# A hybrid layer's 32 experts: the home of weight tiles changes from 12 fixed tiles to a ring of 16

## What is computed

```python
def moe_ffn(h, w_router, b_router, w_gu, b_gu, w_down, b_down):
    logits = (h @ w_router + b_router).astype(F32)
    top_val, top_idx = lax.top_k(logits, TOP_K)          # TOP_K = 4
    gate = jax.nn.softmax(top_val, axis=-1)
    ...
    def expert_block(args):
        xb, e = args
        gu = xb @ w_gu[e] + b_gu[e]                      # 1024 x 2048
        gt = jnp.minimum(gu[:, :D_FF], SWIGLU_LIMIT)
        up = jnp.clip(gu[:, D_FF:], -SWIGLU_LIMIT, SWIGLU_LIMIT)
        act = gt * jax.nn.sigmoid(SWIGLU_ALPHA * gt) * (up + 1.0)
        return act @ w_down[e] + b_down[e]               # 1024 x 1024
```

## Time and profile before

| what | value |
|---|---|
| median of 3 runs | 1384.24 us (1382.01 to 1384.98) |
| profiled execution, its own time | 1385.36 us |
| its span on the core | 1383.4 us, mean granted TensorE clock 0.985 |
| PE busy | 1306.0 us, 94% |
| DVE, ACT, POOL busy | 465.5, 211.8, 20.8 us |
| moved by DMA | 440.18 MB, 318 GB/s over the span |
| expert refills | from 434.69 us on |

### The profile page before, as it was taken

The page is one execution under the profiler, slowest core; times in us unless marked ns, Lnnn a source line. Parts: engine busy times, 40 slices in busy tenths (PEclk is TensorE's granted clock), DMA queues, the critical chain, the costliest instruction groups (busy, mean ns, idle before and its releaser), DMA issues.

```text
span 1383.4 us, 21763 instructions
## 1 busy us (share of the span) xinstructions
PE 1306.0 (94%) x8567; PEld 582.1 (42%) x8567; DVE 465.5 (34%) x983; ACT 211.8 (15%) x556; POOL 20.8 (2%) x30
## 2 busy tenths in 40 slices
PE   5999989999998999999999999999999999999997
PEld 4677544467644343334333333333333333333332
DVE  2454153352535332233222332222332222233223
ACT  3541232460332000000000000000000000000000
POOL 0000010200000000000000000000000000000000
PEclk9999979999998999999999999999999999999999
DMA  9511000365105899999999999999999999999996
GB/s 335 194 62 63 1 28 16 152 219 208 69 6 208 344 422 422 422 422 422 422 422 422 422 422 422 422 422 422 422 422 422 422 422 422 422 422 422 422 421 276
DMA packets 75064, 440.18 MB, mean 318 GB/s; under 512 B 10147, under 2 KB 12681, under 8 KB 25782
## 3 DMA queue, kind: packets, MB, share of 16 engines
q1 hardware_dynamic: 74940, 439.64, 77.7%
q10 hardware_dynamic: 90, 0.06, 0.0%
HBM read 436.35 MB, written 3.33 MB: 318 GB/s over the span
## 4 chain that ended last, share of the span: by engine, by line
PE 50%; DMA 43%; DVE 3%; ACT 2%; issue 1%; SPq 1%; POOL 0%; DVEq 0%; POOLq 0%; ACTq 0%
PE bank L983 47%; DMA weights<-in_w_gu 42%; PE bank L986 2%; SPq L494 1%; ACT weights L572 1%; ACT scaled L572 1%; DMA x<-in_x_sample 0%; ACT stream L572 0%; DVE x L2252 0%; DVE x L2095 0%; POOL stats L545 0%; ACT hT L572 0%; DVE scaled L1698 0%; DVE x L1694 0%; DVE stream L1694 0%
## 5 line engine op out<-in xcount | busy, mean ns | idle before, releaser
L983 PE MATMUL bank<-weights,small_weights 128*64 128x512 f32 x2048 | 480.6, 600 | 24.0 <-DMA weights<-in_w_gu 20.3
L2252 DVE SCALAR_TENSOR_TENSOR x<-bank,small_weights,x 128x512 f32<-128x512 f32 (+1 forms) x192 | 134.8, 743 | 599.8 <-PE bank L983 599.8
L983 PEld LDWEIGHTS bank<-weights,small_weights 128*64 128x64 f32 x2048 | 131.4, 136 | 341.0 <-issue 194.3
L983 PE MATMUL bank<-weights,scaled 128*64 128x512 f32 x1024 | 226.8, 595 | 7.5 <-ACT scaled L572 7.5
L983 PEld LDWEIGHTS bank<-weights,scaled 128*64 128x64 f32 x1024 | 70.7, 137 | 141.5 <-issue 127.9
L572 ACT ACTIVATE scaled<-bank 128x256 f32<-128x256 f32 (+5 forms) x153 | 58.2, 408 | 356.1 <-PE bank L983 264.6
L983 PE MATMUL bank<-scaled,small_weights 64*128 64x512 f32 x384 | 108.1, 640 | 1.4 <-DVE x L2252 0.7
L572 ACT ACTIVATE scaled<-scaled 128x512 f32<-128x512 f32 x32 | 20.2, 630 | 563.0 <-DVE scaled L1698 563.0
L983 PEld LDWEIGHTS bank<-mem_kv,stream 128*128 128x128 bf16 x2376 | 74.3, 100 | 29.4 <-issue 25.2
L983 PE MATMUL bank<-mem_kv,stream 128*128 128x64 bf16 x2376 | 78.2, 196 | 3.3 <-DVE stream L1694 2.5
L983 PE MATMUL bank<-hT,weights 128*128 128x320 f32 (+1 forms) x272 | 76.6, 437 | 0.6 <-ACT hT L572 0.6
(11 more groups left out here) (205 smaller groups left out, 865.8 us busy)
## 6 DMA issues: line engine op xcount, KB each, us to landing
weights<-in_w_gu SPq DMA_DIRECT2D x256, 1024.0 KB, 25.9
weights<-in_w_down SPq DMA_DIRECT2D x128, 1024.0 KB, 24.6
weights<-in_w_in SPq DMA_DIRECT2D x4, 2048.0 KB, 14.6
stream<-in_w_out SPq DMA_DIRECT2D x2, 2048.0 KB, 9.8
weights<-in_w_in SPq DMA_DIRECT2D x1, 2816.0 KB, 18.7
x<-in_x_prompt SPq DMA_DIRECT2D x2, 1024.0 KB, 5.7
weights<-in_w_mk SPq DMA_DIRECT2D x1, 2048.0 KB, 9.6
weights<-in_w_mv SPq DMA_DIRECT2D x1, 2048.0 KB, 8.3
```

The source lines that it names most:

```text
L983: return pe.matmul(out, lhsT, rhs, start=start, stop=stop)
L2252: dve.scalar_tensor_tensor(xx, PS[bank][0:rows, :], gcur[0:rows, b:b + 1], xx, ALU.mult, ALU.add)\
```

## The change

The 12 fixed homes become a ring of 16. Twelve are `weights` cut in pieces of 2048 columns; four more lie in tiles that are no longer read by then: `small_weights` (R, columns 1280 to 3327), `mem_kv` (KV, 1280 to 3327), `stream` (V, 6144 to 8191) and `hT` (HM, 0 to 2047). Tile n of all 384, counted in the order of use, lives in home n modulo 16. PE counts one semaphore, `tile_used`, in place of `gu_used` and `dn_used`, and the refill with tile n waits until n - 15 tiles have been used. Since 12 tiles per expert and 16 homes meet again after four experts, PE's loop has four experts per pass (7 passes, experts 1 to 28; 29 to 31 are written out) and SP's loop has 48 refills per pass (7 passes; the last 32 are written out). The four tiles 12 to 15, the first of expert 1, are loaded ahead of the stage. To have enough semaphores, four loads share one with another load (`ld_mem`, `ld_kcache`, `ld_wmq` go; their waits name the sum), and `gateT` moves from `stream` to `mem_kv`.

```diff
-        gu_sb = W[:, 0:16384].rearrange("p (k n) -> p k n", k=KD)
-        dn_sb = W[:, 16384:24576].rearrange("p (k n) -> p k n", k=KD)
+        TILES, SLOTN, TURN = KD + KD // 2, 16, 4
+        slot_sb = [W[:, 2 * FF * n:2 * FF * (n + 1)] for n in range(12)] + \
+            [R[:, 1280:3328], KV[:, 1280:3328], V[:, 6144:8192], HM[:, 0:2048]]
+        def tile_at(n):
+            return slot_sb[n % SLOTN], f"ld_slot{n % SLOTN}", 16 * (n // SLOTN + 1)
+        def turned(i, c):
+            return [(ap, name, i * (16 * TURN * TILES // SLOTN) + count)
+                    for ap, name, count in (tile_at(TILES * (1 + c) + t) for t in range(TILES))]
...
-        gateT = V[0:E, 5888:6272]
+        gateT = KV[0:E, 3328:3712]
...
-            load(mem3, b_major(mem_prompt[0]), "ld_mem")
+            load(mem3, b_major(mem_prompt[0]), "ld_gn")
...
-            first_gate_up(0, 2)
+            first_tiles(0, 2)
+            sp.wait_ge(sem("att_o"), ATT["mem"] + H * TB)
+            first_tiles(TILES, TILES + 2)
             sp.wait_ge(sem("x3_mm"), 2 * TB)
-            first_gate_up(2, 4)
+            first_tiles(2, 4)
+            first_tiles(TILES + 2, TILES + 3)
+            sp.wait_ge(sem("lg_mm"), TB)
+            first_tiles(TILES + 3, SLOTN)
...
-            gate_up_loads(0, 1)
-            down_loads(0, 1)
-            with sp.Fori(1, E - 1) as it:
-                gate_up_loads(it, it + 1)
-                down_loads(it, it + 1)
+            def refill(n, i):
+                sp.wait_ge(sem("tile_used"), i * (TURN * TILES) + (n - SLOTN + 1))
+                dst, name, _ = tile_at(n)
+                sp.dma_start(dst, tile_rows(bass.ds(i * TURN + n // TILES, 1), n % TILES, False)).then_inc(sem(name), 16)
+            with sp.Fori(0, (E - 2) // TURN) as i:
+                for n in range(SLOTN, SLOTN + TURN * TILES):
+                    refill(n, i)
+            for n in range(SLOTN + (E - 2) // TURN * TURN * TILES, E * TILES):
+                sp.wait_ge(sem("tile_used"), n - SLOTN + 1)
+                dst, name, _ = tile_at(n)
+                sp.dma_start(dst, tile_rows(n // TILES, n % TILES, True)).then_inc(sem(name), 16)
...
-                act.wait_ge(sem("ld_mem"), 16)
+                act.wait_ge(sem("ld_gn"), 128)
...
-                act.wait_ge(sem("dn_used"), it * (KD // 2) + KD // 2)
+                act.wait_ge(sem("tile_used"), it * TILES + TILES)
...
-                    pe.wait_ge(sem(f"ld_gu{k}"), it * 16 + 16)
+                    pe.wait_ge(sem(tiles[k][1]), tiles[k][2])
                     part(k, 0)
-                    part(k, 1).then_inc(sem("gu_used"), 1)
+                    part(k, 1).then_inc(sem("tile_used"), 1)
...
-            with pe.Fori(1, E) as it:
+            def expert(it, tiles):
                 pe.wait_ge(sem("xg_ready"), it + 1)
-                gate_up(it, it - 1)
+                gate_up(it, tiles, it - 1)
                 gather(it + 1)
-                down(it)
+                down(it, tiles)
+            with pe.Fori(0, (E - 2) // TURN) as i:
+                for c in range(TURN):
+                    expert(i * TURN + (1 + c), turned(i, c))
+            for e in range(1 + (E - 2) // TURN * TURN, E):
+                expert(e, fixed(e))
...
-                dve.wait_ge(sem("gu_used"), it * KD + KD)
+                dve.wait_ge(sem("tile_used"), it * TILES + KD)
```

More of the change, by code:

```diff
@@ L469, in _, with tile_rows, first_tiles @@
                 load(braw[32 * n:32 * n + 32, :], b_gu[0], "ld_bias")
-            def first_gate_up(k0, k1):
-                for k in range(k0, k1):
-                    load(gu_sb[:, k, :], w_gu[0, 0, k * P:(k + 1) * P, :], f"ld_gu{k}")
+            def tile_rows(e, t, first):
+                if t < KD:
+                    w = w_gu[0, e, t * P:(t + 1) * P, :]
+                    return w if first else w.rearrange("a p n -> p (a n)")
+                k = t - KD
+                w = w_down[0, e, 2 * k * P:(2 * k + 2) * P, :]
+                return w.rearrange("(p k) n -> p (k n)" if first else "a (p k) n -> p (a k n)", k=2)
+            def first_tiles(t0, t1):
+                for t in range(t0, t1):
+                    load(slot_sb[t], tile_rows(t // TILES, t % TILES, True), f"ld_slot{t}")
             sp.wait_ge(sem("st_conv"), 32)
             sp.wait_ge(sem("st_mk"), 32)
-            first_gate_up(4, KD)
+            first_tiles(4, KD)
             sp.wait_ge(sem("att_o"), ATT["mem"])
-            for k in range(KD // 2):
-                load(dn_sb[:, 2 * k:2 * k + 2, :], w_down[0, 0, 2 * k * P:(2 * k + 2) * P, :]
-                     .rearrange("(p k) n -> p k n", k=2), f"ld_dn{k}")
+            first_tiles(KD, TILES)
             sp.wait_ge(sem("x2_mm"), KD)
@@ L525, in _ @@
                     e = sp.value_load(xlist[0:1, bass.ds(j, 1)], min_val=0, max_val=E - 1)
-                    gate_up_loads(j + (E - 1), e)
-                    down_loads(j + (E - 1), e)
+                    sp.wait_ge(sem("tile_used"), j * TILES + E * TILES)
+                    for t in range(TILES):
+                        sp.dma_start(slot_sb[t], tile_rows(bass.ds(e, 1), t, False)).then_inc(sem(f"ld_slot{t}"), 16)
                 sp.wait_ge(*at("y_final"))
@@ L1591, in gather, with gate_up @@
                 m.then_inc(sem("slots_tr"), 1)
-            def gate_up(it, before=None, between=None):
+            def gate_up(it, tiles, before=None, between=None):
                 pe.wait_ge(sem("sel_ready"), it + 1)
@@ L1619, in gate_up, with down @@
                 for k in (KD - 2, KD - 1):
-                    part(k, 1).then_inc(sem("gu_used"), 1)
+                    part(k, 1).then_inc(sem("tile_used"), 1)
                 if between is not None:
                     between(KD - 2)
-            def down(it):
+            def down(it, tiles):
                 pe.wait_ge(sem("act_ready"), it * 2 + 2)
@@ L1638, in down @@
                             m = mm(PS[3][64 * half:64 * half + 64, :], actT[:, k % 4, 64 * (k // 4):64 * (k // 4) + 64],
-                                   dn_sb[:, k, 512 * half:512 * half + 512], k == 0, k == KD - 1)
-                    m.then_inc(sem("dn_used"), 1)
+                                   tiles[KD + n][0][:, FF * (k % 2) + 512 * half:FF * (k % 2) + 512 * half + 512],
+                                   k == 0, k == KD - 1)
+                    m.then_inc(sem("tile_used"), 1)
             def scatter(it, b, bank=6, free=None):
@@ L1658, in _ @@
             pe.wait_ge(sem("b3_step"), 6)
-            gate_up(0, between=between_first)
+            gate_up(0, fixed(0), between=between_first)
             pe.wait_ge(sem("y0_add"), 2 * TB)
@@ L1676, in _ @@
                     pe.wait_ge(sem("xg_ready"), j + (E + 2))
-                    gate_up(j + E)
-                    down(j + E)
+                    gate_up(j + E, extra(j))
+                    down(j + E, extra(j))
                     for b in range(TB):
@@ L1933, in scan_b @@
                 if s:
[L1934 removed]
+                    dve.wait_ge(sem("ld_state"), 64)
                 if c:
```

39 lines of the change are left out of this document (16 added, 23 removed).

## The result

| what | before | after |
|---|---|---|
| median of the runs | 1384.91 us (9 runs, 1382.01 to 1390.32) | 1376.59 us (9 runs, 1374.11 to 1383.54) |
| ratio, with its 95% interval | | 0.9942 (0.9923 to 0.9961) |
| profiled execution, its own time | 1385.36 us | 1375.59 us |
| its span | 1383.4 us | 1373.8 us |

The kernel became 8.3 us faster, inside the predicted range and 2.3 us above the point named. It was measured three more times, on two chips (two of the three are runs with register moves further down, which turn out to be the same program): 0.9959 (0.9943 to 0.9974), 0.9956 (0.994 to 0.9972) and 0.9938 (0.9916 to 0.9961), medians 1378.2 to 1378.7 us. The mean of the four ratios is 0.9949, or 7.1 us.

The account below looks back on a forecast made before the run. Saturated expert-tile transfers at 422 GB/s were taken to bound the kernel. Four tiles fewer to move gave -9.94 us, all other terms 0: from the median 1384.24 us to 1374.3 us, range 1371.5 to 1379 us.

Parts of the forecast that it names:

- What bounds the kernel: Expert stage: saturated transfers at 422 GB/s need 29.82 us per expert, PE 28.02 us; expert 31's eighth tile sets the end.
- the size of the gain: Expert stage: 368 tiles follow the first refill instead of 372, four times 2.485 us, 9.94 us off.
- Why the four count: Ahead of the expert stage: four tiles land before the first refill at 434.69; each us it comes later delays the end.
- The early dip stays: Transfers at 440 to 460 us: 349 GB/s stays, as a ring of 16 has nothing to request there; no gain.
- PE can follow: Expert stage: without waits PE reaches expert 31's eighth tile at 1322.5, its landing allows 1350.7; 28.2 us to spare.
- Loops, waits and counters at 0: PE, SP and the merged counters: same matmuls, one wait per tile, SP's work per tile as before; cost 0.
- Rival 1: PE's longer loop is fetched again at six branches, s each (1322.5 + 6 s): 1377.3 us (0.07) or 1502 us (0.05).
- near price: Stall per branch back of PE's loop: 0.96 us packet time plus 4.2 us, 5.2 us; 1377.3 us, chance 0.07.
- Rivals 2, 3 and 4: 2: PE's pace grows, 1384 us (0.05). 3: dip fills, 1367.4 us (0.03). 4: first refill after 434.69, within the range's width.

Follow-up runs that it names:

- runs with register moves: Changed kernel with 130 or 256 register moves ahead of PE's first instruction, which the build drops: 1378.73 us and 1378.21 us.
- hold: Changed kernel, but SP holds the first refill until PE has used eight tiles: 1386.98 us, ratio 1.0012 to the kernel before.
- the late four: Changed kernel, but tiles 12 to 15 are asked for only at PE's first use of a tile: 1380.63 us, ratio 0.9967 to the kernel before.
- the run with the drains: Changed kernel with 130 drains (instructions that compute nothing) ahead of PE's first work: 1395.94 us, ratio 1.0075 to the kernel before.

## Why the prediction was right, and where not

- **What bounds the kernel, and the size of the gain.** Right: four tiles at 2.485 us. 9.94 us were predicted for the eighth tile of expert 31, 9.92 came; 22.8 us were to stand behind it, 23.1 do. 15 or 16 waits were expected, 17 came. That it fits to 0.02 us is luck: in the three other traces of the changed kernel the eighth tile came 6.8 to 9.2 us earlier than in before. In the first one 48 GB/s more than before moved between 390 and 490 us, worth 11.4 us, where four tiles are 42 GB/s, and the terms below took the surplus away again.
- **Why the four count.** Wrong in its words, though the sum came out. They do not count because they are ahead of the first refill, and a later first refill is not a later end us by us: 17.96 us of hold moved the eighth tile by 12.1, and asking for the four at the first refill cost 2 to 4 us, not 9.9. They count because 265 instead of 217 GB/s move between 390 and 490 us, in time that stood idle. By the prediction's reason the loads ahead of 434 us had to be early; in fact any place from which they move before the transfers are saturated does nearly as well, as the late four show.
- **The early dip stays.** Right: 340 GB/s after 349 in 440 to 460.
- **PE can follow, with 28.2 us to spare.** Right. In the run with the drains PE lost 47.8 us on six branches; the last eighth tile came only 17.1 us later than in after (1367.75 for 1350.69), so some 30.7 us were there to be lost.
- **Loops, waits and counters at 0.** Mis-sized by some 1 to 2 us. The sum of window and eighth tile is 1413.0 to 1413.9 with the loops of four and 1412.0 before; twelve homes with the new loops have a ratio of 1.0016 to before, with an interval that still holds 1. The first pass brings seven or eight q8 packets and one q14 packet into the saturated stage. The prediction named these packets as a sign and gave them no price; with one for each of eight engines, at 1.45 us, an estimate is 1.5 us. It would explain a part of why the medians gained 5 to 8 us, not 9.94; the rest is open.
- **Rival 1.** The mechanism is real, and stayed away by the place of the loop, which nobody had chosen: that was luck. Its near price of 5.2 us a branch was too low for the moved loop; 8.0 was measured, which by the rival's own formula is slower than before. The prediction asked whether seven packets fit, a question of size; where the loop stands it didn't ask. The wait at a branch is not the whole: a second stall and a lower granted clock come on top. That packets of code hold up single DMA engines and with them the tiles, so that a fetch costs time even with PE's stall hidden, was left out of it.
- **Rivals 2, 3 and 4** did not come: PE is 99.22 of 100 us busy between 600 and 700 as before, the dip did not fill, and the first refill stood at 434.54.

## What to carry to other kernels

Where transfers run saturated to the end, count what they have moved by the time they become so: the end follows that number, and it matters little which request came first. It holds as long as no DMA engine is held up by something else: then the slowest engine sets the end, though hardly less is moved. After any change of a hardware loop or of the code ahead of it, look in the trace at the instruction queues behind the first pass; a loop near the limit can be fetched anew in each pass because of instructions added far ahead of it, and the bill is a stall at each branch and late tiles besides.

## What the hardware did that was not expected

- 130 instructions ahead of PE's program made a loop of 1576 instructions, unchanged in itself, cost 8.0 us per branch back: 60 packets for 8, and 17 us of the whole kernel.
- A packet of code costs the saturated tiles far more than its bytes at the full rate (0.04 us for 16 KB, 0.02 us for 8 KB): 39 packets on q8 cost 7.1 us and 12 on q14 6.3 us. When the tiles ran out, eight, one and (with both) nine of the 16 DMA engines were behind the others.
- SP's loop of 48 refills stays, that of 96 doesn't (13 packets on q14 for 1).
- Holding the first refill up by 18 us costs 12 in the profiled execution and 8 to 10 by the medians, since the queue that builds up fills the dip behind it: 424 for 376 GB/s between 460 and 480 us.
